# A Strassen-type SwiGLU stage on one Trainium2 core: gate/up and down products merged into one block

## The chip, the cores and the metric

The program runs on one core of one Trainium2 chip. It is one launch; the time is the device time of that launch in microseconds (us). The engines named below are TensorE (PE, matmuls, with its weight loads as PEld), VectorE (DVE), ScalarE (ACT), GpSimd (POOL) and SyncE (SP, which here only issues transfers). Each runs its own list of instructions in order and meets the others through semaphores.

## The reference

One layer of an encoder trunk is applied to two requests of 2048 and 512 tokens with 1024 features. In short:

```
u = rmsnorm(h) ; z = u @ w_in                       # input projection
a, p, f = short conv with gates, multiscale pool, 2-D Fourier transform of parts of z
h = h + concat(rms(a), rms(p), rms(f)) * mix_g @ w_out
v = rmsnorm(h)
gate, up = split(v @ w_gate_up)                     # 1024 -> 2 * 2816
h = h + (silu(gate) * up) @ w_down                  # 2816 -> 1024
out = rmsnorm(h)                                    # without the 16 meta tokens
```

All of it is in 32-bit floats. The change touches only the last three lines: the two products of the feed-forward part, the product of `silu(gate)` and `up` between them, and the final norm.

## The kernel before

**Three matmuls for one.** Every large product is done with operands split into a high part (type fp32r, an ACT copy) and a low part (what is left, a DVE subtraction). `split_product` (lines 79 to 83) issues hi·hi, hi·lo and lo·hi, which are the lines L81, L82 and L83 of all rows below.

**Seven products for eight.** Both feed-forward products cut their matrices in 2 x 2 and use seven products (`FORMS = 7`, numbered 0 to 6) of sums of quadrants. The summed weights (`gu_sums`, `down_sums`) are made beforehand in HBM by accumulating transfers that POOL issues in eight "waves" (class `Forms`). The sums of `v`, the normed activations, are made on chip: `v_raw` holds the quadrants A11, A21, A22, A12 and one sum, and DVE makes four subtractions in it in place (`v_sum`), named D, N6, E and S3.

**`gateup`** (from L1463). The tokens come in three "halves" of 428, 428 and 424 columns. For each half there are 11 iterations of two output tiles y = 0 and 1, so 33 iterations; each has 14 units, ordered by form and then by y. A unit is one form of one tile: 12 matmuls of 428 columns. SP loads one 256 KB weight block per unit into a ring of eight (`gu_raw`); ACT makes `gu_hi` and DVE makes `gu_lo`, six units ahead of PE. In a new half ACT and DVE also make `v_form_hi` and `v_form_lo` of each of the seven forms (`v_split`, 1712 columns each), and DVE the four sums. These big steps are put in the last iteration of the half before, one form after another. ACT and DVE also read the accumulators out (`read_out`): s1 is a copy of form 0; u2, u3, c22, c12, c21 are DVE sums of accumulators; then two SiLUs on ACT, two products (`act_left`, `act_right`) and four sums (`act_sums`) on DVE. POOL stores seven forms of the result to `act_forms` in HBM. PE waits where an accumulator is used again, or where the next form is added onto it: form 3 waits for u2, form 4 for s1, form 5 for c22, form 6 for u3.

**`down`** (from L1720) is a block of its own: it begins when all engines have left `gateup`. It has 3 groups of token tiles (4, 3 and 3 tiles of 128 tokens per side), 77 units each: for a unit SP loads 256 KB of weights (`down_raw`) and up to 256 KB of activations (`act_raw`), ACT and DVE split both, PE does 12 (or 9) matmuls of 512 columns, and DVE adds the seven accumulated forms onto the residual rows `h_tiles`. After the first eight units' loads SP issues the load of `final` and the eight first residual tiles (L1837, L1853), and only then the loads of the ninth unit. ACT, POOL and DVE do the final norm, POOL stores the rows.

The order of the work on every engine is written out by hand by these loops; no scheduler moves anything.

Of the kernel before, what the change touches and what calls it, by code (L numbers as in the profile page):

```python
# [1462 lines left out]
def gateup(nc, c, gu, dn, w_landed):  # L1463

    HM, SLOTS, AHEAD = max(HALVES), UNIT_RING, 6
    ITER, UNITS = GU_ITER, GU_UNITS
    A11, A21, A22, A12, AX = range(5)
    D_, N6, E_, S3 = range(1, 5)
    a_of, b_of, c_of = (lambda y: 3 * y), (lambda y: 3 * y + 1), (lambda y: 3 * y + 2)
    ACC = (a_of, b_of, c_of, b_of, a_of, c_of, b_of)
    with ExitStack() as ctx:
        sb = lambda n, s, d=F32: ctx.enter_context(nc.sbuf_tensor(n + "_sb", s, d))
        sem = lambda n: ctx.enter_context(nc.semaphore(n))
        vf_hi, vf_lo = (sb(n, [P, FORMS, 4, HM], F32R) for n in ("v_form_hi", "v_form_lo"))  # L1480
        vraw = sb("v_raw", [P, 5, 4, HM])
# [628 lines left out]
```

## Time and profile before

| what | us |
|---|---|
| median of 3 runs (lowest, highest) | 2551.2 (2550.27, 2556.29) |
| the profiled execution, its own time | 2553.51 |
| its span from first to last instruction | 2551.9 |
| PE busy in it | 2398.7 (94%) |
| DVE busy | 1550.0 (61%) |
| ACT busy | 893.4 (35%) |
| POOL busy | 359.6 (14%) |

The span is 1.6 us shorter than the execution's own time: what lies around it. The stages follow each other: input projection up to about 475 us, Fourier transform to 600, output projection to 868, gate/up from 897 to 1983, down from 2007 to about 2540, and the end of the final norm and the last stores to 2552. A busy share says that an engine works, not that it sets the time; what sets it in a stage is the engine for which nothing else waits, and its idle stretches are what a change can win.

### The profile page before, as it was taken

The page shows a single profiled execution, that of the slowest core. Times are in us where ns is not written, and L with a number is a line of the kernel's source. Part 1 is how long each engine was busy: PE and PEld are TensorE (multiplying, and loading weights), DVE is VectorE, ACT ScalarE, POOL GpSimd, SP SyncE. Part 2 cuts the span into 40 slices and gives each one's busy share as a digit, 9 for nine tenths or more (in the row PEclk, how much of TensorE's full clock was granted, in tenths as well). Part 3 has the DMA queues.
Part 4 walks back from the last instruction along what each step waited for, and adds up shares of the span by engine and source line. Part 5 has one row for each costly group of instructions (what it writes and reads, how often), then busy time and mean ns, then how long its engine had stood idle before and what let it go on. Part 6 is the DMA issues. An engine that isn't in the chain of part 4 may idle for free. (4 is left out here: it accounts for less than half of the span.)

```text
span 2551.9 us, 32577 instructions
## 1 busy us (share of the span) xinstructions
PE 2398.7 (94%) x11786; PEld 2150.5 (84%) x11786; DVE 1550.0 (61%) x2312; ACT 893.4 (35%) x1486; POOL 359.6 (14%) x509
## 2 busy tenths in 40 slices
PE   6999999788999589999999999999999599999997
PEld 4887888677888489999999999999999488888886
DVE  4443545555877375555865555856555375686875
ACT  4121211142443243333433333433333243454543
POOL 0110110006444001111010011111111000110101
PEclk9999999887999799999999999999999799999999
DMA  5656871265565547888555455455553786687874
GB/s 179 215 134 161 220 201 52 91 208 190 210 251 199 187 142 259 259 251 250 163 192 199 159 163 161 155 164 160 163 160 118 251 281 192 207 311 225 260 242 139
DMA packets 216058, 492.95 MB, mean 193 GB/s; under 512 B 27552, under 2 KB 60866, under 8 KB 207469
## 3 DMA queue, kind: packets, MB, share of 16 engines
q1 hardware_dynamic: 188301, 358.99, 43.0%
q0 software_dynamic: 27616, 132.11, 17.3%
q8 instruction: 85, 1.39, 0.2%
q14 instruction: 56, 0.46, 0.1%
HBM read 395.90 MB, written 164.31 MB: 220 GB/s over the span
## 5 line engine op out<-in xcount | busy, mean ns | idle before, releaser
L81 PE MATMUL gu_bank<-v_form_hi_sb,gu_hi_sb 128*128 128x428 f32 (+1 forms) x1848 | 658.5, 356 | 37.7 <-DVE gu_lo_sb L1604 29.8
L82 PE MATMUL gu_bank<-v_form_lo_sb,gu_hi_sb 128*128 128x428 f32 (+1 forms) x1848 | 658.0, 356 | 0.0
L83 PE MATMUL gu_bank<-v_form_hi_sb,gu_lo_sb 128*128 128x428 f32 (+1 forms) x1848 | 657.9, 356 | 0.0
L1604 DVE TENSOR_TENSOR gu_lo_sb<-gu_raw_sb,gu_hi_sb 128x512 fp32r<-128x512 f32 x462 | 313.8, 687 | 208.3 <-ACT gu_hi_sb L1556 208.3
L81 PEld LDWEIGHTS gu_bank<-v_form_hi_sb,gu_hi_sb 128*128 128x128 f32 x1848 | 347.3, 188 | 51.2 <-DVE gu_lo_sb L1604 38.2
L1556 ACT ACTIVATE gu_hi_sb<-gu_raw_sb 128x512 fp32r<-128x512 f32 x462 | 281.3, 627 | 254.9 <-PE gu_bank L83 246.8
L82 PEld LDWEIGHTS gu_bank<-v_form_lo_sb,gu_hi_sb 128*128 128x128 f32 x1848 | 347.5, 188 | 11.2
L83 PEld LDWEIGHTS gu_bank<-v_form_hi_sb,gu_lo_sb 128*128 128x128 f32 x1848 | 347.5, 188 | 10.7
L81 PE MATMUL down_bank<-down_hi_sb,act_hi_sb 128*128 128x512 f32 x770 | 301.0, 391 | 27.6 <-DVE act_lo_sb L1943 27.6
L82 PE MATMUL down_bank<-down_lo_sb,act_hi_sb 128*128 128x512 f32 x770 | 300.5, 390 | 0.0
L83 PE MATMUL down_bank<-down_hi_sb,act_lo_sb 128*128 128x512 f32 x770 | 300.5, 390 | 0.0
L1940 DVE TENSOR_TENSOR down_lo_sb<-down_raw_sb,down_hi_sb 128x1024 fp32r<-128x1024 f32 x116 | 141.7, 1222 | 170.2 <-ACT down_hi_sb L1892 169.6
L1892 ACT ACTIVATE down_hi_sb<-down_raw_sb 128x1024 fp32r<-128x1024 f32 x116 | 122.9, 1060 | 296.7 <-PE down_bank L83 238.3
L81 PE MATMUL proj_bank<-u_hi_sb,w_in_hi_sb 128*128 128x512 f32 x480 | 188.6, 393 | 7.7 <-DVE u_lo_sb L459 6.7
L81 PEld LDWEIGHTS down_bank<-down_hi_sb,act_hi_sb 128*128 128x128 f32 x770 | 145.2, 189 | 58.5 <-DVE down_lo_sb L1940 28.3
L82 PE MATMUL proj_bank<-u_lo_sb,w_in_hi_sb 128*128 128x512 f32 x480 | 187.9, 391 | 0.0
L83 PE MATMUL proj_bank<-u_hi_sb,w_in_lo_sb 128*128 128x512 f32 x480 | 187.7, 391 | 0.0
L1541 POOL DMA_DIRECT2D act_forms<-act_left_sb x66 | 36.4, 551 | 984.2 <-DVE act_sums_sb L1654 984.2
L83 PEld LDWEIGHTS down_bank<-down_hi_sb,act_lo_sb 128*128 128x128 f32 x770 | 145.1, 188 | 30.4
L82 PEld LDWEIGHTS down_bank<-down_lo_sb,act_hi_sb 128*128 128x128 f32 x770 | 145.2, 189 | 30.1
L81 PE MATMUL out_bank<-w_panel_hi_sb,v_hi_sb 128*128 128x512 f32 x320 | 128.4, 401 | 5.5 <-DVE h_sb L1347 5.5
L1943 DVE TENSOR_TENSOR act_lo_sb<-act_raw_sb,act_hi_sb 128x384 fp32r<-128x384 f32 (+1 forms) x231 | 132.3, 599 | 0.7 <-ACT act_hi_sb L1899 0.5
(187 smaller groups left out, 3293.2 us busy)
## 6 DMA issues: line engine op xcount, KB each, us to landing
gu_raw_sb<-gu_sums SPq DMA_DIRECT2D x264, 256.0 KB, 3.9
gu_raw_sb<-w_gu_q SPq DMA_DIRECT2D x198, 256.0 KB, 2.6
gu_sums<-w_gu_q POOLq DMA_DIRECT2D x24, 1408.0 KB, 14.4
down_raw_sb<-down_sums SPq DMA_DIRECT2D x132, 256.0 KB, 3.7
act_raw_sb<-act_forms SPq DMA_DIRECT2D x154, 192.0 KB, 3.6
down_raw_sb<-w_down_q SPq DMA_DIRECT2D x99, 256.0 KB, 3.3
w_raw_sb<-w_panels SPq DMA_DIRECT2D x40, 512.0 KB, 3.5
act_raw_sb<-act_forms SPq DMA_DIRECT2D x77, 256.0 KB, 4.3
```

Source lines behind the costliest of these rows:

```text
L81: pe.matmul(out, w[0], x[0], start=first, stop=False, skip_group_check=True)
L82: pe.matmul(out, w[0], x[1], start=False, stop=False, skip_group_check=True)
L83: return pe.matmul(out, w[1], x[0], start=False, stop=last, skip_group_check=True)
L1541: pool.dma_start(c["act_forms"][f, m, :, at:at + n], src[:, 0:n]).then_inc(a_stored, 16)
L1556: act.activation(w_hi[:, s, :], raw[:, s, :], ACT.Copy).then_inc(w_hi_made, 1)
L1604: dve.tensor_tensor(w_lo[:, s, :], raw[:, s, :], w_hi[:, s, :].bitcast(F32), ALU.subtract)\
L1892: act.activation(w_hi[:, s:e, :], w_raw[:, s:e, :], ACT.Copy).then_inc(w_hi_made, 1)
L1940: dve.tensor_tensor(w_lo[:, s:e, :], w_raw[:, s:e, :], w_hi[:, s:e, :].bitcast(F32), ALU.subtract)\
L1943: dve.tensor_tensor(a_lo[:, s, 0:w], a_raw[:, s, 0:w], a_hi[:, s, 0:w].bitcast(F32), ALU.subtract)\
```

## The change

`gateup` and `down` become one function, `swiglu`, with one block. What it does:

- The weight ring (`gu_raw`, `gu_hi`, `gu_lo`) serves both products, with semaphores counted on. The buffers that only the down product needs lie over buffers that only gate/up needs: `act_raw` and `act_hi` over `v_raw`, `act_lo` over the first forms of `v_form_lo`, the residual tiles `h_even` over `v_form_hi`, `h_odd` and `final` over the rest of `v_form_lo`. So the loads and splits of the first down units stand in the lists of SP, ACT and DVE right behind the last gate/up units, and the loads of `final` and `h_even` wait until PE has done all gate/up units.
- The seventh product (form 6) has its own bank for each y (`g_of`), and the order of the forms is 0, 4, 6, 1, 2, 3, 5 (`TURN`). The read-out of c21 moves from behind form 6 to behind form 3, between u3 and c22; form 5 comes directly behind form 3. The form's sign change is gone, so its low part is a plain subtraction.
- The four loads of `v` are issued one by one (A11, two weight blocks, A12, two weight blocks, A21 and A22; in later halves in iterations 2, 4, 6 and 8), and each has its own semaphore. D and N6 are made after form 4's split, E after form 6's, S3 after form 1's; before, D, N6 and E all stood behind form 0's.
- The waves of the `w_down` sums are issued one piece in each of 16 iterations, where before there were two pieces in each of 8.
- The accumulators of the down product are mapped to other banks (`acc`), so that the first form's do not meet the last ones of gate/up.

The core of the diff:

```diff
-    ACC = (a_of, b_of, c_of, b_of, a_of, c_of, b_of)
+    g_of = lambda y: 6 + y
+    ACC = (a_of, b_of, c_of, b_of, a_of, c_of, g_of)
+    TURN = (0, 4, 6, 1, 2, 3, 5)
+    AT = tuple(TURN.index(f) for f in range(FORMS))
...
+            for u in range(GU_UNITS):
...
+                if u == 1:
+                    v_load(0, A12)
+                elif u == 3:
+                    v_load(0, A21)
+                    v_load(0, A22)
+                if i % HF in V_LOAD_AT and f == 0 and y == 0 and i // HF + 1 < len(HALVES):
+                    sp.wait_ge(v_lo_made, FORMS * (i // HF + 1))
+                    v_load(i // HF + 1, V_LOAD_AT[i % HF])
...
+                sp.wait_ge(w_lo_made, w_lo_by(u - SLOTS))
+                sp.dma_start(raw[:, slot(u), :], down_weights(u)).then_inc(w_landed[slot(u)], 16)
...
+                if u == SLOTS - 1:
+                    sp.wait_ge(used, GU_UNITS)
+                    sp.dma_start(gf[:, :], c["final_rows"]).then_inc(gf_landed, 16)
+                    h_load(0)
...
-                if 1 <= i <= 8:
-                    for piece in range(dn.pieces):
-                        dn.wave(pool, i - 1, piece)
+                if 1 <= i <= 8 * dn.pieces:
+                    dn.wave(pool, (i - 1) // dn.pieces, (i - 1) % dn.pieces)
...
             def v_step(k, f):
 
                 v_split(k, f)
-                if f == 0:
+                if f == 4:
                     v_sum(k, D_)
                     v_sum(k, N6)
+                elif f == 6:
                     v_sum(k, E_)
                 elif f == 1:
                     v_sum(k, S3)
...
                 elif f == 3:
                     dve.wait_ge(used, u + 1)
-                    dve.tensor_tensor(u3[:, y, 0:n], acc, s1[:, y, 0:n], ALU.subtract).then_inc(u3_made, 1)
+                    dve.tensor_tensor(u3[:, y, 0:n], there, s1[:, y, 0:n], ALU.subtract).then_inc(u3_made, 1)
                     dve.wait_ge(u3_made, now)
+                    dve.tensor_tensor(s1[:, y, 0:n], bank[:, g_of(y), 0:n], u3[:, y, 0:n], ALU.subtract).then_inc(c21_made, 1)
+                    dve.wait_ge(c21_made, now)
                     dve.tensor_tensor(u3[:, y, 0:n], bank[:, c_of(y), 0:n], u3[:, y, 0:n], ALU.add).then_inc(c22_made, 1)
...
-                elif f == 6:
-                    dve.wait_ge(used, u + 1)
-                    dve.tensor_tensor(s1[:, y, 0:n], s1[:, y, 0:n], acc, ALU.subtract).then_inc(c21_made, 1)
...
             def w_split(u):
-                if u >= UNITS:
+                if u >= GU_UNITS:
+                    splits(u - GU_UNITS)
                     return
```

Three places show how the lists change. First ACT, in its order, at the beginning of gate/up, from the fourth form's high part on (`s1_sb<-gu_bank` is the copy of form 0's accumulator; `gu_used` is PE's count of finished units). Before:

```order
L1565 ACTIVATE v_form_hi_sb<-v_raw_sb 128x1712 [waits v_landed]
L1556 ACTIVATE gu_hi_sb<-gu_raw_sb 128x512 [waits unit_landed6]
L1575 ACTIVATE s1_sb<-gu_bank 128x428 [waits gu_used]
L1556 ACTIVATE gu_hi_sb<-gu_raw_sb 128x512 [waits unit_landed7]
L1575 ACTIVATE s1_sb<-gu_bank 128x428 [waits gu_used]
```

And after:

```order
L1724 ACTIVATE v_form_hi_sb<-v_raw_sb 128x1712 [waits v_summed] x4
L1714 ACTIVATE gu_hi_sb<-gu_raw_sb 128x512 [waits unit_landed6]
L1733 ACTIVATE s1_sb<-gu_bank 128x428 [waits gu_used]
L1714 ACTIVATE gu_hi_sb<-gu_raw_sb 128x512 [waits unit_landed7]
L1733 ACTIVATE s1_sb<-gu_bank 128x428 [waits gu_used]
L1714 ACTIVATE gu_hi_sb<-gu_raw_sb 128x512 [waits gu_used,unit_landed0]
L1738 ACT_TABLE_LOAD
```

The copy s1 stands behind all seven high parts in both. What moved is who waits for it: before it was the ninth and tenth unit of PE (form 4), now it is the third and fourth.

Second DVE, in the last iteration of a half, where the next half's forms are made (`v_raw_sb<-v_raw_sb` are the sums D, N6, E, S3; L1663 and L1863 are u2; L1666 and L1866 are u3; L1668 and L1870 are c22; L1868 is c21). Before:

```order
L1663 TENSOR_TENSOR u_sb<-gu_bank,s_sb 128x428
L1626 TENSOR_TENSOR v_form_lo_sb<-v_raw_sb,v_form_hi_sb 128x1712
L1616 TENSOR_TENSOR v_raw_sb<-v_raw_sb 128x1712 x3
L1604 TENSOR_TENSOR gu_lo_sb<-gu_raw_sb,gu_hi_sb 128x512
L1663 TENSOR_TENSOR u_sb<-gu_bank,s_sb 128x428
L1604 TENSOR_TENSOR gu_lo_sb<-gu_raw_sb,gu_hi_sb 128x512
L1626 TENSOR_TENSOR v_form_lo_sb<-v_raw_sb,v_form_hi_sb 128x1712
L1616 TENSOR_TENSOR v_raw_sb<-v_raw_sb 128x1712
L1604 TENSOR_TENSOR gu_lo_sb<-gu_raw_sb,gu_hi_sb 128x512 x2
L1666 TENSOR_TENSOR u_sb<-gu_bank,s_sb 128x428
L1668 TENSOR_TENSOR u_sb<-gu_bank,u_sb 128x428
```

And after, from the second form's low part to c22 of y = 0:

```order
L1824 TENSOR_TENSOR v_form_lo_sb<-v_raw_sb,v_form_hi_sb 128x1712
L1818 TENSOR_TENSOR v_raw_sb<-v_raw_sb 128x1712 x2
L1806 TENSOR_TENSOR gu_lo_sb<-gu_raw_sb,gu_hi_sb 128x512 x2
L1863 TENSOR_TENSOR u_sb<-gu_bank,s_sb 128x428
L1824 TENSOR_TENSOR v_form_lo_sb<-v_raw_sb,v_form_hi_sb 128x1712
L1818 TENSOR_TENSOR v_raw_sb<-v_raw_sb 128x1712
L1806 TENSOR_TENSOR gu_lo_sb<-gu_raw_sb,gu_hi_sb 128x512
L1863 TENSOR_TENSOR u_sb<-gu_bank,s_sb 128x428
L1806 TENSOR_TENSOR gu_lo_sb<-gu_raw_sb,gu_hi_sb 128x512
L1824 TENSOR_TENSOR v_form_lo_sb<-v_raw_sb,v_form_hi_sb 128x1712
L1818 TENSOR_TENSOR v_raw_sb<-v_raw_sb 128x1712
L1806 TENSOR_TENSOR gu_lo_sb<-gu_raw_sb,gu_hi_sb 128x512 x2
```

behind which, with nothing between:

```order
L1866 TENSOR_TENSOR u_sb<-gu_bank,s_sb 128x428
L1868 TENSOR_TENSOR s_sb<-gu_bank,u_sb 128x428
L1870 TENSOR_TENSOR u_sb<-gu_bank,u_sb 128x428
L1824 TENSOR_TENSOR v_form_lo_sb<-v_raw_sb,v_form_hi_sb 128x1712
L1806 TENSOR_TENSOR gu_lo_sb<-gu_raw_sb,gu_hi_sb 128x512
```

The two u2 stand further back against the new forms, and all four sums and four low parts now lie ahead of the first c22.

Third SP, at the end of gate/up. Before (the two branches are the end of one block and the beginning of the next):

```order
L1528 DMA gu_raw_sb<-gu_sums 128x512 x2
L1477 UNCONDITIONAL_BRANCH
L1828 UNCONDITIONAL_BRANCH
L1847 DMA down_raw_sb<-w_down_q 128x512
L1850 DMA act_raw_sb<-act_forms 128x512
```

And after:

```order
L1625 DMA gu_raw_sb<-w_gu_q 128x512 x2
L1652 DMA gu_raw_sb<-w_down_q 128x512
L1660 DMA act_raw_sb<-act_forms 128x512
```

The branches are gone and the loads of the first down units follow the last of gate/up. The load of `final` (L1664) and the eleven pieces of the residual tiles (L1643) still stand between the loads of the eighth and of the ninth down unit.

## Rows read from the trace of the kernel before

**Rows 1.** The page, costliest groups: shapes, count | busy us, mean ns | idle before, releaser.
```profile
L1556 ACT ACTIVATE gu_hi_sb<-gu_raw_sb 128x512 fp32r<-128x512 f32 x462 | 281.3, 627 | 254.9 <-PE gu_bank L83 246.8
```

**Rows 2.** Waits of PE: line, released by; us in total, times, longest.
```profile
PE gu_bank L81 <- DVE u_sb L1663: 6.6, 5, 2.8
...
PE gu_bank L81 <- DVE u_sb L1668: 1.3, 2, 0.7
```

**Rows 3.** Timeline, beginning of gate/up: start, duration, instruction, idle before.
```profile
875.75 2.24 SPq L1519 DMA_DIRECT2D v_raw_sb<-vT  x4
...
887.54 1.63 ACT L1565 ACTIVATE v_form_hi_sb<-v_raw_sb 128x1712 fp32r<-128x1712 f32 x1 [19.08 <-DMA v_raw_sb<-vT]
...
889.20 1.94 DVE L1626 TENSOR_TENSOR v_form_lo_sb<-v_raw_sb,v_form_hi_sb 128x1712 fp32r<-128x1712 f32 x1 [22.84 <-ACT v_form_hi_sb L1565]
891.06 5.76 DVE L1616 TENSOR_TENSOR v_raw_sb<-v_raw_sb 128x1712 f32<-128x1712 f32 x3
...
897.48 0.72 PE L81 MATMUL gu_bank<-v_form_hi_sb,gu_hi_sb 128*128 128x428 f32 x1 [29.76 <-DVE gu_lo_sb L1604]
...
915.87 0.43 PE L81 MATMUL gu_bank<-v_form_hi_sb,gu_hi_sb 128*128 128x428 f32 x1 [2.77 <-DVE u_sb L1663]
```

**Rows 4.** Windows: stretch, length; busy PE, PEld, DVE, ACT, POOL; clock, DMA share, GB/s.
```profile
877.90:887.10 9.20, 0.00 (x0) 0.00 (x0) 0.00 (x0) 0.00 (x0) 0.00 (x0) 0.50 1.04 385
897.48:900.50 3.02, 3.02 (x9) 2.81 (x10) 3.02 (x3) 3.02 (x5) 0.00 (x0) 0.50 0.55 174
913.10:915.87 2.77, 0.00 (x1) 0.03 (x1) 2.77 (x6) 0.63 (x1) 0.00 (x0) 1.00 0.19 48
```

**Rows 5.** Timeline, change from the first half to the second.
```profile
1252.79 0.53 ACT L1580 ACTIVATE silu_sb<-gu_bank 128x428 f32<-128x428 f32 x1 [1.28 <-PE gu_bank L83]
...
1255.00 0.60 DVE L1668 TENSOR_TENSOR u_sb<-gu_bank,u_sb 128x428 f32<-128x428 f32 x1
...
1255.75 0.43 PE L81 MATMUL gu_bank<-v_form_hi_sb,gu_hi_sb 128*128 128x428 f32 x1 [0.68 <-DVE u_sb L1668]
```

**Rows 6.** Timeline, read-out of form 3 in the middle of gate/up, DVE.
```profile
1508.73 0.60 DVE L1666 TENSOR_TENSOR u_sb<-gu_bank,s_sb 128x428 f32<-128x428 f32 x1 [3.23 <-PE gu_bank L83]
...
1509.37 0.60 DVE L1668 TENSOR_TENSOR u_sb<-gu_bank,u_sb 128x428 f32<-128x428 f32 x1
...
1509.89 0.68 DVE L1604 TENSOR_TENSOR gu_lo_sb<-gu_raw_sb,gu_hi_sb 128x512 fp32r<-128x512 f32 x1
...
1511.05 0.60 DVE L1666 TENSOR_TENSOR u_sb<-gu_bank,s_sb 128x428 f32<-128x428 f32 x1 [0.47 <-PE gu_bank L83]
```

**Rows 7.** Timeline, from gate/up to down.
```profile
2006.62 0.43 SPq L1853 DMA_DIRECT2D final_sb<-final_rows  x1
...
2007.48 0.77 PE L81 MATMUL down_bank<-down_hi_sb,act_hi_sb 128*128 128x512 f32 x1 [24.90 <-DVE act_lo_sb L1943]
...
2031.87 1.06 ACT L1892 ACTIVATE down_hi_sb<-down_raw_sb 128x1024 fp32r<-128x1024 f32 x1 [16.81 <-DMA act_raw_sb<-act_forms]
...
2034.94 0.47 PE L81 MATMUL down_bank<-down_hi_sb,act_hi_sb 128*128 128x512 f32 x1 [2.72 <-DVE act_lo_sb L1943]
```

**Rows 8.** Windows of the same place, columns as in rows 4.
```profile
2006.62:2031.87 25.25, 24.39 (x96) 19.90 (x96) 8.61 (x12) 6.30 (x9) 0.00 (x0) 0.87 1.04 336
1998.27:2006.62 8.35, 0.00 (x0) 0.00 (x0) 1.11 (x1) 2.10 (x3) 0.00 (x0) 0.50 0.85 276
1986.00:1993.00 7.00, 0.00 (x0) 0.00 (x0) 0.69 (x2) 0.00 (x0) 3.74 (x7) 0.50 0.60 217
2007.48:2012.90 5.42, 5.42 (x13) 4.26 (x14) 4.45 (x6) 4.20 (x6) 0.00 (x0) 0.50 1.06 404
...
2040.00:2060.00 20.00, 20.00 (x90) 16.56 (x89) 19.02 (x29) 10.47 (x15) 0.00 (x0) 1.00 0.85 303
```

**Rows 9.** An idle stretch of PE in the input projection and the clock behind it.
```profile
228.83 1.97 PE L628 MATMUL proj_bank<-ident_sb,x_tiles_sb 128*128 128x128 f32 x8 [4.25 <-DVE u_lo_sb L459]
228.83:238.10 9.27, 7.68 (x22) 6.08 (x23) 1.92 (x3) 1.20 (x2) 0.00 (x0) 0.50 0.67 244
```

More of the change, by code:

```diff
@@ L1460, in _, with row_ranges, swiglu @@
             transposes(NBLK - 1, 24 * (NBLK - 1) + 16)
-def gateup(nc, c, gu, dn, w_landed):
+def row_ranges(pair, right):
+    out, lo = [], P * pair
+    for at, n, token in zip(SEQ_AT, HALVES, TOKEN_AT):
+        a, b = max(lo, at), min(lo + P, at + n)
+        if a < b:
+            out.append((a - lo, b - lo, token + a - at + (n if right else 0)))
+    return out
+def swiglu(nc, c, gu, dn, half, eps):
     HM, SLOTS, AHEAD = max(HALVES), UNIT_RING, 6
-    ITER, UNITS = GU_ITER, GU_UNITS
+    ITER, UNITS = GU_ITER, FORMS * HF
+    ALL = UNITS * len(PAIRS)
     A11, A21, A22, A12, AX = range(5)
@@ L1510, in gateup, with slot, unit_landed, w_lo_by @@
         V_SUM = (0, N6, E_, D_, 0, S3, 0)
+        V_LOAD_AT = {2: A11, 4: A12, 6: A21, 8: A22}
+        def slot(u):
+            return (GU_UNITS + u) % SLOTS
+        def unit_landed(u):
+            earlier = len(range(slot(u), GU_UNITS, SLOTS))
+            return 16 * earlier + 32 * ((GU_UNITS + u) // SLOTS + 1 - earlier)
+        def w_lo_by(u):
+            return GU_UNITS + (u // 2 if u >= 0 else u) + 1
+        def acc(g, i):
+            return bank[:, ((6, 7, 0, 3), (2, 5, 1, 4))[g % 2][i], :]
@@ L1523, in _, with v_load @@
-            v_load(0)
+            def v_load(k, where):
+                n = HALVES[k]
+                row, at = {A11: (0, 0), A21: (0, n), A22: (512, n), A12: (512, 0)}[where]
+                sp.dma_start(vraw[:, where, :, 0:n], c["vT"][row:row + 512, TOKEN_AT[k] + at:TOKEN_AT[k] + at + n]
+                             .rearrange("(k p) n -> p k n", p=P)).then_inc(v_landed[where], 16)
+            v_load(0, A11)
             gu.all_made(sp)
-            for u in range(UNITS):
+            for u in range(GU_UNITS):
@@ L1595, in _ @@
                     v_split(i // HF + 1, f)
+            for u in range(ALL):
+                k, v = divmod(u, UNITS)
+                splits(u + AHEAD)
+                if 70 <= v < 70 + PAIRS[k][1]:
+                    square_rows(k, 0, v - 70)
+                if k and 4 <= v < 4 + PAIRS[k - 1][1]:
+                    square_rows(k - 1, 1, v - 4)
+            for i in range(PAIRS[-1][1]):
+                square_rows(len(PAIRS) - 1, 1, i)
         @block.vector
@@ L1599, in w_split @@
             def w_split(u):
-                if u >= UNITS:
+                if u >= GU_UNITS:
+                    splits(u - GU_UNITS)
                     return
@@ L1613, in v_sum @@
                     dve.wait_ge(v_summed, 4 * k + what - 1)
-                else:
-                    dve.wait_ge(v_landed, 64 * (k + 1))
+                for where in {D_: (A11, A21), N6: (A22,), E_: (), S3: (A12,)}[what]:
+                    dve.wait_ge(v_landed[where], 16 * (k + 1))
                 dve.tensor_tensor(part(out), part(x), part(y), ALU.subtract).then_inc(v_summed, 1)
@@ L1658, in read_out @@
                 n, now = HALVES[i // HF], 2 * i + y + 1
-                acc = bank[:, ACC[f](y), 0:n]
+                there = bank[:, ACC[f](y), 0:n]
                 if f == 1:
@@ L2018, in build @@
             outproj(nc, c, feed, ident, half, eps)
-        landed = [ctx.enter_context(nc.semaphore(f"unit_landed{i}")) for i in range(UNIT_RING)]
-        gateup(nc, c, gu, dn, landed)
-        down(nc, c, dn, landed, half, eps)
+        swiglu(nc, c, gu, dn, half, eps)
 def dft_tables(length, rows, freqs):
```

457 lines of the change are left out of this document (208 added, 249 removed).

## The prediction

> **What bounds the kernel now.** I read the busy shares first: PE 94%, DVE 61%, so most of the time is PE's own, and only PE's idle stretches and its slow clock can be won. Then PE's waits, longest first. Two stand out, both between stages: 29.76 us before the first gate/up matmul [rows 3] and 24.90 us before the first down matmul [rows 7]. Behind these come 2.77 us at the seventh gate/up unit [rows 3], 2.72 us at the ninth down unit [rows 7], and small waits for u2 and c22 [rows 2]: 6.6 + 1.3 us, less the 2.77, is 5.1 us, all at the two changes of half. Everywhere else in gate/up and down PE waits for nothing. The clock adds to both large waits: it restarts at 0.50, that is 1.2 of 2.4 GHz, for 3.02 us in gate/up [rows 4] and for 5.42 us in down [rows 8], which loses half of that, 1.5 and 2.7 us.
>
> So two units of time serve below. A gate/up unit takes 2.32 to 2.33 us (read-outs of neighbouring units start 2.32 apart [rows 6]); a down unit of four tiles takes 2.66 (90 matmuls in 20 us, twelve to the unit [rows 8]).
>
> **From gate/up to down (gain).** PE's last gate/up matmul ends at 2007.48 - 24.90 = 1982.58. Now the first eight down units are loaded and split by then: their weights follow in a ring that ran eight units ahead, their activations are those of the first two halves, stored long ago, and the banks they need are read out by form 5 of the tile. PE goes on without a gap, at full clock, and the eight units end 8 x 2.66 = 21.3 us later. Then the ninth. Its loads stand on SP behind `final` and eleven pieces of residual tiles, 4.7 MB, and these now wait for PE's last gate/up matmul, because the buffers lie over `v_form_hi` and `v_form_lo`. Before, from the issue of `final` at 2006.62 to the split of the ninth unit's operands at 2031.87 were 25.25 us at 336 GB/s, 8.5 MB [rows 7, 8]. In it were 1.9 MB left from the sixteen loads of 4.2 MB, of which 2.3 MB had moved (8.35 us at 276 GB/s); these are now gone. New is the store of the last iteration's seven act forms, 7 us at 217 GB/s, 1.5 MB, which before had ended when down began [rows 8] and now runs beside the residual tiles. So 8.1 MB, 24.1 us at the same rate, and 3.1 from the split to PE's start (2031.87 to 2034.94 [rows 7]): the ninth unit starts 27.3 us after the last gate/up matmul, a stall of 6.0 us. At 404 GB/s, the best rate seen there [rows 8], it would be 23.2 us, a stall of 1.9. A stall of 6 us also drops the clock, which after 4.25 idle us was at 0.50 [rows 9]; I take 2.0 us for the restart, between 1.5 and 2.7. Before, the ninth unit came 2034.94 - 1982.58 = 52.4 us after; now 29.3. Gain 23.1 us; 29 at best, 20 at worst (rate 300 GB/s).
>
> The Trainium skill, "DMA: Bandwidth & Descriptors", section "Queues, rings and completion order", says that each transfer engine takes turns between the queues that have work for it. By this the stores of POOL's queue share with SP's loads; if instead they ran only behind them, the ninth unit would come 1.5 MB earlier and the stall would be about 1.5 us. No row of before has both at once at this place.
>
> **The beginning of gate/up (no gain).** Here the words of the change promise most: PE can start when A11 has landed. The four v loads moved at 385 GB/s from 877.9 to 887.1 [rows 4], and ACT took them up at 887.54 [rows 3]. A11 alone (0.88 MB) lands at about 880.7, ACT's high part takes 1.63, DVE's low part 1.94, then one weight block: PE starts at about 885 instead of 897.48. But form 4 now comes second and is added onto form 0's bank, so PE's third unit waits for s1, and in ACT's list s1 stands behind all seven high parts. The last of them waits for S3 on DVE. DVE's chain: A22 now has four weight blocks ahead of it and lands at 877.9 + 4.56 MB / 385 GB/s + 0.5 = 890.2. Behind it N6 1.92, two weight splits 1.2, low part 1.86, E 1.92, two splits 1.2, low part 1.86, S3 1.94 (back-to-back instructions overlap by 0.08: 889.20 to 891.06 for 1.94 [rows 3]) end at 902.1. ACT: high part 1.63, one weight part 0.6 [rows 1], s1 0.5, and 0.2 to PE: 905. PE has had two units and idles some 13 us, so the clock is at half again. The seventh unit starts four units later, 905 + 9.3 + 2.0 for the clock = 916.4; before it was at 915.87 [rows 3]. Its own wait for u2 is gone, since form 1 comes there. Cost 0.5 us; between 4 lost (A22 later, clock 2.7) and 3 won (A22 as before).
>
> **Changes of half (loss).** Before, DVE was late by 5.1 us in both together. Now follow DVE in the last tile of a half, from its first unit's start T. ACT gets to form 4's high part when the fourth unit is done: 4 x 2.33 = 9.3, 0.2 to see it, a SiLU 0.45, high part 1.53, weight part 0.6, DVE's weight split 0.6: DVE begins form 4's low part at T + 12.8. From there to c22 of y = 0 stand, by the order shown, three low parts 5.6, four sums 7.6, six weight splits 3.6, two u2 1.0, and u3, c21, c22 with 0.64, 0.64 and 0.60 [rows 6]: 19.7 us. PE needs it 0.2 later (1255.60 to 1255.75, and a first matmul of 0.43 [rows 5]): T + 32.7. The unit that waits (form 5, y = 0) is the thirteenth and due at T + 28.0: 4.6 us late. Its twin waits for c22 of y = 1: 0.52, low part 1.86, split 0.6, 1.9 for three read-outs, less 0.6 and less a unit: 1.9 us. Together 6.5 for each change, where 2.6 were; the same reckoning for before gives 3.1 where 2.6 is measured, so I take 6.2. If the 4.6 us also drop the clock, the slow unit mostly hides in the second wait; 0.4 for that. Two changes: 13.2 against 5.1, 8.1 us lost. Bounds: 3 lost, if ACT delivers earlier, and 14, if the clock falls for 9.27 us as in rows 9.
>
> The Trainium skill, "TensorE: Matmul & The Clock Gate", section "HAM oscillation — how this bites in real kernels", warns that waits between bursts of matmuls drop the clock again each time. This speaks against a change that turns many short waits into a few of 4 to 13 us. Rows 9 agree for 4.25 us; 2.77 us left the clock at 1.00 [rows 4]. By this rule the second half-change wait costs more and the sum would be some 3 us worse.
>
> **Every other iteration (near nothing, but on a knife's edge).** c22 now has u3 and c21 ahead of it and only one unit's time. u3 starts 0.22 after the next unit does: the wait at 1255.75 began at 1255.07, a free successor starts 0.17 before that end, a unit earlier is 1252.57, and ACT's read-out there began at 1252.79 [rows 5]. c22 of y = 0 ends 0.22 + 1.88 = 2.10 into the unit, PE has it at 2.32 of 2.33. For y = 1 a weight split comes between: 0.22 + 1.28 + 0.52 + 0.60 + 1.88 = 4.50, plus 0.23 = 4.73 of 4.66: 0.07 late, 33 times 2 us in all. Taken 2; bounds 0 and, with 0.3 lost in each of 66 units, 20.
>
> **Nothing by themselves:** the spread v loads of later halves (they end four iterations before use), the spread waves of the `w_down` sums (PE has no wait there [rows 2]), the plain subtraction for form 6 (1.94 either way), the bank map, fewer SP instructions. The waves' cover is some sixteen further iterations of 32 us.
>
> **Sum.** 23.1 - 0.5 - 8.1 - 2.0 = 12.5 us. The profiled execution took 2553.5 (span 2551.9 and 1.6 around it), so 2541.0 for that one; it lay 2.3 above the median of the runs, 2551.2, which gives 2538.7. I forecast 2539 us.
>
> **Rivals.**
> 1. *The front work is hidden after all.* Half changes cost no more than before and the start wins 3, the stall of the ninth unit is 2 us. For it: DVE is 61% busy only, and the sums are spread. Against it: in the order all four sums stand ahead of the first c22. 29 + 3 - 1 = 31 at most, 2520; typically 2524.
> 2. *The ninth unit and its followers.* The 8.1 MB move at 276 GB/s, as the first down loads did [rows 8]: the ninth unit comes 32.5 us after the last gate/up matmul, and the next pairs stall 2 us more. For it: DMA share 1.04 there [rows 8]. Against it: the 336 measured with the same tiles. Gain only 52.4 - 32.5 - 4 = 16, and 10 to 14 lost in gate/up: 2545 to 2549.
> 3. *Slower: the c22 chain.* If u3 to c22 takes 0.3 to 0.6 us longer than rows 6 let expect, because the weight split ahead of u3 isn't done when the unit ends, each of 66 units of form 5 waits that long: 20 to 40 us, against 14.5 won elsewhere. From 0.22 us per unit the gain is gone; at 0.45 the time is 2567. For it: the margin is 0.01 us. Against it: ACT has the weights two units ahead.
> 4. *It doesn't do what it says*: down still starts after a gap, since one of the shared buffers is released late. Then the 24.9 us stay and 2560 follows.
>
> **How the numbers follow.** Forecast 0.56 (2531 to 2544), rival 1 0.18, rival 2 0.15, rival 3 0.07, rival 4 0.04. Range 2526 to 2548, which leaves out the better half of rival 1 and most of 3 and 4. About 0.3%, 7.7 us, can be told from no change. Faster by more (below 2543.5): all of rival 1, nearly all of the forecast and a little of rival 2, 0.76; within it: the rest of these, and the mild end of rival 3, 0.16; slower 0.08.
>
> **What would show it.** In the profile after: no PE wait at the first down unit and one of 2 to 8 us, for act_lo, at the ninth; two early units at about 885, then some 13 us of wait for s1, and the seventh unit at 914 to 919; two pairs of waits for c22 of about 4.5 and 1.9 us; no other wait over 0.2 us in gate/up. Half-change waits under 3 us, or an s1 wait that is missing, would make the forecast too high; waits of 0.3 us in every iteration, too low.

## The result: faster by a little over a quarter of a per cent, and the profile after

| | kernel before | kernel after |
|---|---|---|
| median of 20 runs (lowest, highest), us | 2554.73 (2547.02, 2562.26) | 2547.03 (2540.06, 2557.29) |
| the profiled execution, us | 2553.51 | 2544.79 |
| ratio, with its 95% interval | | 0.9973 [0.9963, 0.9982] |

The gain is 7.7 us by the medians and 8.7 by the two profiled executions; 12.5 were forecast. The time forecast, 2539, is 8 us too low: 3.5 of that are the kernel before, whose three first runs had their median at 2551.2 and whose twenty have it at 2554.7; the rest, 12.5 less 7.7, is an error of the sum.

PE's longest waits after the change (line, released by: us in total, times, longest). They answer to [rows 2] and to the waits in [rows 3, 7]:

```profile
PE gu_bank L81 <- DVE gu_lo_sb L1806: 17.3, 1, 17.3
...
PE gu_bank L81 <- ACT s_sb L1733: 13.7, 1, 13.7
PE gu_bank L81 <- DVE u_sb L1870: 9.2, 4, 4.4
...
PE gu_bank L81 <- DVE act_lo_sb L1898: 3.5, 1, 3.5
```

The wait of 24.90 us before down is gone, and the one of 29.76 before gate/up is now two, 17.3 and 13.7. The same waits on the timeline, with the first down matmul:

```profile
906.67 0.69 PE L81 MATMUL gu_bank<-v_form_hi_sb,gu_hi_sb 128*128 128x428 f32 x1 [13.72 <-ACT s_sb L1733]
...
918.19 0.36 PE L81 MATMUL gu_bank<-v_form_hi_sb,gu_hi_sb 128*128 128x428 f32 x1
...
1263.20 0.70 PE L81 MATMUL gu_bank<-v_form_hi_sb,gu_hi_sb 128*128 128x428 f32 x1 [4.36 <-DVE u_sb L1870]
...
1993.80 0.35 PE L83 MATMUL gu_bank<-v_form_hi_sb,gu_lo_sb 128*128 128x424 f32 x1
1993.99 0.39 PE L81 MATMUL gu_bank<-gu_hi_sb,act_hi_sb 128*128 128x512 f32 x1
...
2019.66 0.47 PE L81 MATMUL gu_bank<-gu_hi_sb,act_hi_sb 128*128 128x512 f32 x1 [3.52 <-DVE act_lo_sb L1898]
```

918.19 is the seventh unit, which now follows without a wait. The clock behind these waits (columns as in [rows 4]):

```profile
906.67:912.00 5.33, 5.33 (x17) 5.01 (x18) 4.62 (x5) 3.27 (x6) 0.00 (x0) 0.56 0.13 33
1263.20:1270.00 6.80, 6.55 (x25) 5.92 (x26) 6.70 (x9) 0.89 (x2) 0.00 (x0) 0.77 0.32 95
1628.78:1636.00 7.22, 7.22 (x23) 6.63 (x24) 7.12 (x9) 0.89 (x2) 0.00 (x0) 0.57 0.31 92
2019.66:2026.00 6.34, 6.34 (x21) 5.04 (x22) 5.49 (x8) 5.12 (x8) 0.00 (x0) 0.73 1.05 386
```

And the row that the forecast had nothing for. Down in mid-flow, no wait in it and the clock at 1.00 throughout; first the kernel before, then the one after:

```profile
2200.00:2250.00 50.00, 50.00 (x222) 41.39 (x221) 35.72 (x45) 28.45 (x49) 13.79 (x24) 1.00 0.79 253
2300.00:2350.00 50.00, 50.00 (x222) 41.42 (x221) 32.30 (x47) 23.05 (x37) 0.00 (x0) 1.00 0.73 229
```

```profile
2200.00:2250.00 50.00, 50.00 (x220) 41.02 (x219) 40.72 (x56) 26.31 (x44) 12.46 (x20) 1.00 0.76 255
2300.00:2350.00 50.00, 50.00 (x220) 41.04 (x219) 31.84 (x46) 23.20 (x37) 0.00 (x0) 1.00 0.73 225
```

222 matmuls in 50 us before, 220 after. Averaged over the start times of a longer stretch, one follows the other in 226.7 ns before and 228.9 after; below this is called the distance. The engine is busy all the time in both, so neither busy time nor waits show it; only the counts in equal windows do. Over the 2,214 matmuls from the ninth unit on it is 4.9 us.

**The account of the 8.7 us** by which the two profiled executions differ, from the times of PE's rows:

| stretch | us won |
|---|---|
| stages ahead of gate/up (nothing differs there: chance) | -0.6 |
| beginning of gate/up (seventh unit at 918.19, where it was 915.87, less the 0.6) | -1.7 |
| from the seventh unit to the end of gate/up (1075.8 us up to the first down matmul at 1993.99, before 1066.7) | -9.1 |
| from there to the ninth down unit (25.7 us, before 52.4) | +26.7 |
| slow clock behind that (6.34 us at 0.73) | -1.7 |
| distance of the down matmuls | -4.9 |

### The profile page after: what moved, and what is told of

It reads as the page before. It is cut to its first block and busy times, and to the rows that moved or that the text cites. A ratio compares the mean times of both kernels' runs of the same rounds, so it can differ in the third digit from the quotient of the medians.

```text
span 2543.2 us, 32577 instructions
## 1 busy us (share of the span) xinstructions
PE 2408.1 (95%) x11786; PEld 2151.0 (85%) x11786; DVE 1548.3 (61%) x2312; ACT 903.1 (36%) x1486; POOL 361.0 (14%) x509
## 5 line engine op out<-in xcount | busy, mean ns | idle before, releaser
L81 PE MATMUL gu_bank<-v_form_hi_sb,gu_hi_sb 128*128 128x428 f32 (+1 forms) x1848 | 663.2, 359 | 40.2 <-DVE gu_lo_sb L1806 17.3
L81 PE MATMUL gu_bank<-gu_hi_sb,act_hi_sb 128*128 128x512 f32 x770 | 303.9, 395 | 3.5 <-DVE act_lo_sb L1898 3.5
L83 PE MATMUL gu_bank<-gu_hi_sb,act_lo_sb 128*128 128x512 f32 x770 | 302.4, 393 | 0.0
L82 PE MATMUL gu_bank<-gu_lo_sb,act_hi_sb 128*128 128x512 f32 x770 | 299.7, 389 | 0.0
L1893 DVE TENSOR_TENSOR gu_lo_sb<-gu_raw_sb,gu_hi_sb 128x1024 fp32r<-128x1024 f32 x116 | 141.4, 1219 | 157.2 <-ACT gu_hi_sb L1750 157.2
L1750 ACT ACTIVATE gu_hi_sb<-gu_raw_sb 128x1024 fp32r<-128x1024 f32 x116 | 122.5, 1056 | 295.4 <-PE gu_bank L83 258.3
L83 PEld LDWEIGHTS gu_bank<-gu_hi_sb,act_lo_sb 128*128 128x128 f32 x770 | 145.0, 188 | 33.9
L81 PEld LDWEIGHTS gu_bank<-gu_hi_sb,act_hi_sb 128*128 128x128 f32 x770 | 145.2, 189 | 33.0 <-DVE gu_lo_sb L1893 3.9
L82 PEld LDWEIGHTS gu_bank<-gu_lo_sb,act_hi_sb 128*128 128x128 f32 x770 | 144.8, 188 | 32.3
```

The costliest lines, as they stand in the source:

```text
L81: pe.matmul(out, w[0], x[0], start=first, stop=False, skip_group_check=True)
L82: pe.matmul(out, w[0], x[1], start=False, stop=False, skip_group_check=True)
L83: return pe.matmul(out, w[1], x[0], start=False, stop=last, skip_group_check=True)
L1750: act.activation(w_hi[:, s:e, :], raw[:, s:e, :], ACT.Copy).then_inc(w_hi_made, 1)
L1893: dve.tensor_tensor(w_lo[:, s:e, :], raw[:, s:e, :], w_hi[:, s:e, :].bitcast(F32), ALU.subtract)\
```

## The experiments

The stages ahead of gate/up end up to 9 us apart from run to run, though nothing in them differs. So I compare, beside the medians, the stretch from PE's last row of 32 transposes in the output projection to the end of the span. The two rows, before and after:

```profile
862.29 5.42 PE L1423 MATMUL out_bank<-ident_sb,stage_sb 128*128 128x128 f32 x32 [2.04 <-DVE stage_sb L1354]
```

```profile
862.93 5.40 PE L1423 MATMUL out_bank<-ident_sb,stage_sb 128*128 128x128 f32 x32 [2.04 <-DVE stage_sb L1354]
```

Call the stretch R: 1689.6 us before, 1680.3 after. It comes from the one profiled execution of each kernel.

**1. The kernel before once more.**

> The kernel before, unchanged, profiled once more. In its first profile neighbouring down matmuls start 0.2267 us apart; in the profile of the changed kernel 0.2290 us, which over some 2,200 matmuls is 5 us that my sum did not have. If the kernel sets this distance (its addresses or its accumulator banks), it is 0.2267 here again. If it differs from execution to execution or from chip to chip, it will be another number here, anywhere from 0.226 to 0.230.

2547.43 us, R 1688.0, PE's waits as in [rows 2, 3, 7] within 0.6 us, except 1.40 for 2.77 at the seventh gate/up unit and 1.32 for 2.72 at the ninth down unit; down distance 226.7 ns again. So for this kernel R repeats to 2 us, and the distance to 0.1 ns. For two kernels below the medians say less than R does; both numbers are given there.

**2. The residual tiles two units later.**

```
-                if u == SLOTS - 1:
+                if u == SLOTS + 1:
                     sp.wait_ge(used, GU_UNITS)
                     sp.dma_start(gf[:, :], c["final_rows"]).then_inc(gf_landed, 16)
                     h_load(0)
```

> The changed kernel, but the loads of final and of the first residual tiles stand on SP two units later, behind the loads of the tenth down unit. My account: the wait of 3.5 us at the ninth down unit and the slow clock behind it (1.7 us) go, about 5 us less than the changed kernel, 12 us less than before (ratio to before about 0.9953), unless the eleventh unit waits in their place. Rival: the transfers are limited by bandwidth alone, so the wait only moves two units on and the time stays (0.997). If the layout sets the distance of the down matmuls, it is 0.2290 us here too.

2537.5 us (4 runs), ratio 0.9931 [0.9905, 0.9957], R 1674.2. PE no longer waits in down at all. 6.1 us less than the kernel after in R: the wait of 3.5, the slow clock of 1.7, and 0.9 at the second change of half, where one iteration took 38.75 us here and 39.67 in the kernel after. That 0.9 is chance: with the same order of gate/up experiment 3 had 38.72 there and experiment 7 had 39.77. So the ninth unit did wait behind `final` and the residual tiles, and the whole wait was a matter of order on SP. The distance stays at 228.9.

**3. Down's bank map of before.**

```
-            return bank[:, ((6, 7, 0, 3), (2, 5, 1, 4))[g % 2][i], :]
+            return bank[:, 4 * (g % 2) + i, :]
...
```

PE's waits ahead of the first units of down are adapted to it.

> The changed kernel with the accumulators of the down product in the banks of before (0 to 3 and 4 to 7 in turn), everything else as changed. If the bank map makes the down matmuls slower, their distance goes back from 0.2290 to 0.2267 us and down is 5 us shorter. If the addresses in SBUF or the execution itself do it, 0.2290 stays, or whatever the others of this call show.

2548.69 us, R 1680.6, distance 228.9: the banks have no part in it.

**4. The one block with gate/up's order of before.** `TURN` is 0 to 6, form 6 is back in form 3's bank and last, D, N6 and E stand behind form 0, the four `v` loads of a half go together (each keeps its own semaphore).

```
-    ACC = (a_of, b_of, c_of, b_of, a_of, c_of, g_of)
-    TURN = (0, 4, 6, 1, 2, 3, 5)
+    ACC = (a_of, b_of, c_of, b_of, a_of, c_of, b_of)
+    TURN = (0, 1, 2, 3, 4, 5, 6)
...
-                if f == 4:
+                if f == 0:
                     v_sum(k, D_)
...
```

> Only the merged block: gate/up has its order of before (forms 0 to 6, seventh product in the bank of the second, c21 behind form 6, D, N6 and E behind form 0, the v loads all at once), while rings, overlaid buffers, down banks and spread sums are those of the changed kernel. My account of the two profiles: the order of forms and sums costs 9 to 11 us in gate/up (two changes of half 7, read-outs 1.5, beginning 1 to 2), the merged block wins 25. So this kernel should be 9 to 11 us faster than the changed one and 17 below before, ratio 0.9930 to 0.9940, with waits of about 1.0, 0.7 and 1.0 us at each change of half as before. Rival: the new order costs nothing by itself and the missing gain lies in down; then it is as the changed kernel, 0.997.

2533.8 us (8 runs), ratio 0.9927 [0.9906, 0.9947], R 1663.9. Its rows:

```profile
878.41 1.63 ACT L1720 ACTIVATE v_form_hi_sb<-v_raw_sb 128x1712 fp32r<-128x1712 f32 x1 [12.12 <-DMA v_raw_sb<-vT]
...
888.35 0.72 PE L81 MATMUL gu_bank<-v_form_hi_sb,gu_hi_sb 128*128 128x428 f32 x1 [22.75 <-DVE gu_lo_sb L1803]
...
906.74 0.43 PE L81 MATMUL gu_bank<-v_form_hi_sb,gu_hi_sb 128*128 128x428 f32 x1 [2.53 <-DVE u_sb L1862]
...
1999.38 0.76 PE L81 MATMUL gu_bank<-gu_hi_sb,act_hi_sb 128*128 128x512 f32 x1 [4.10 <-DVE act_lo_sb L1898]
```

At the changes of half PE waits 1.02, 0.69 and 0.96 us, and 0.94, 0.64 and 0.95, as before the change. The new order of gate/up, with its spread loads and the bank of the seventh product, therefore costs 16.4 us of R, two thirds of the 25.7 that this kernel gains on the one before. The medians say less of both: 13.2 us between this kernel and the one after, and by the ratio 19 (14 to 24) against the one before. This profiled execution was a quick one, 2525.39 where the median is 2533.8, so the merge is worth 19 to 26 us and the order costs 13 to 16; experiment 8 has the order alone at 14.

Half of the 16.4 is at the start, which I had put at 0.5: the seventh unit stands 46.8 us behind the row of transposes, 55.3 in the kernel after, and 53.6 in the kernel before. The 6.8 us by which this start beats that of before I put down to the semaphores: ACT takes up A11 18.5 us behind the transposes, at 878.41, when one load has landed; before it was 25.2 us behind, at 887.54 [rows 3], when all four had. These 6.7 us are the whole difference, but no run changes the semaphores alone.

**5. Down's buffers at the places of after, in the kernel before.**

```
-        w_raw, a_raw = (sb(n, [P, SLOTS, UNIT]) for n in ("down_raw", "act_raw"))
-        w_hi, w_lo, a_hi, a_lo = (sb(n, [P, SLOTS, UNIT], F32R) for n in ("down_hi", "down_lo", "act_hi", "act_lo"))
-        h = sb("h_tiles", [P, 2, 2, 4, D])
+        w_raw = sb("down_raw", [P, SLOTS, UNIT])
+        w_hi, w_lo = (sb(n, [P, SLOTS, UNIT], F32R) for n in ("down_hi", "down_lo"))
...
+        sb("gap_1", [P, 9312 // 4])
+        a_raw = sb("act_raw", [P, SLOTS, UNIT])
+        a_hi = sb("act_hi", [P, SLOTS, UNIT], F32R)
+        h_even = sb("h_even", [P, 2, 4, D])
+        sb("gap_2", [P, 16640 // 4])
+        a_lo = sb("act_lo", [P, SLOTS, UNIT], F32R)
...
```

> The kernel before, with the down block's rings and residual tiles at the places in SBUF that they have after the change (weights' high and low parts at 33,696 and 50,080 bytes, activations' at 108,640 and 174,432); nothing else differs. My theory is that these places are what makes the distance between down's matmuls 228.9 ns instead of 226.7: then it is 228.9 here, and the profiled time some 4.8 us above the 2547 to 2553 of the kernel before. The rival: the distance comes with the one block (one long program for PE), whatever the places; then it stays at 226.7 and so does the time.

2553.22 us, R 1693.0, which is 3.4 to 5.0 above the two of before; distance 228.9:

```profile
2200.00:2250.00 50.00, 50.00 (x220) 41.02 (x219) 35.93 (x46) 29.20 (x49) 13.89 (x24) 1.00 0.80 258
2300.00:2350.00 50.00, 50.00 (x220) 41.04 (x219) 31.25 (x45) 23.22 (x37) 0.00 (x0) 1.00 0.71 226
```

The places alone make it. The rival, the one long program, is out: this kernel has the two blocks.

**6. The weights alone at their new place.**

```
-        w_raw, a_raw = (sb(n, [P, SLOTS, UNIT]) for n in ("down_raw", "act_raw"))
-        w_hi, w_lo, a_hi, a_lo = (sb(n, [P, SLOTS, UNIT], F32R) for n in ("down_hi", "down_lo", "act_hi", "act_lo"))
+        w_raw = sb("down_raw", [P, SLOTS, UNIT])
+        w_hi, w_lo = (sb(n, [P, SLOTS, UNIT], F32R) for n in ("down_hi", "down_lo"))
+        a_raw = sb("act_raw", [P, SLOTS, UNIT])
+        a_hi, a_lo = (sb(n, [P, SLOTS, UNIT], F32R) for n in ("act_hi", "act_lo"))
```

> The kernel before, with one change of place in down: the weights' high and low parts at 33,696 and 50,080 bytes, where the kernel after has them, instead of 50,080 and 66,464; the activations' stay at 82,848 and 99,232. If the place of the operand that streams (the weights) sets the distance, it is 228.9 ns; if that of the stationary one (the activations), or the distance of the two, whose offset stays a multiple of 16,384 here, it is 226.7. If the places have no part in it at all, 226.7 too.

2549.16 us, R 1689.7, distance 226.7. Moved by 16,384 bytes, the weights alone change nothing.

**7. The kernel after with two pads.**

```
+        sb("pad_1", [P, 832 // 4])
         with ExitStack() as first:
...
             vf_hi = early("v_form_hi", [P, FORMS, 4, HM], F32R)
+            early("pad_2", [P, 1792 // 4])
             vf_lo = early("v_form_lo", [P, FORMS, 4, HM], F32R)
...
```

> The kernel after, with two pads (832 and 1792 bytes), so that the activations' high and low parts in down stand at a multiple of 2,048 bytes from the weights', as they do in the kernel before (there of 16,384). If what counts is that offset, the distance of down's matmuls falls from 228.9 to 226.7 ns and the time by some 4.8 us, to about 2540. If it is another property of the places, or the one block, it stays at 228.9 and 2545 to 2549.

2541.03 us, R 1675.1: 5.2 less than after, with the same waits (4.37 at the first change of half, 3.94 at the ninth unit). The windows count as before the change:

```profile
2200.00:2250.00 50.00, 50.00 (x222) 41.42 (x221) 40.22 (x54) 26.24 (x44) 12.36 (x20) 1.00 0.78 255
2300.00:2350.00 50.00, 50.00 (x222) 41.42 (x221) 32.90 (x49) 22.74 (x37) 0.00 (x0) 1.00 0.73 228
```

So it is shown from both sides, by 5 and 7, that the place of the activations' buffers makes the difference.

What about the place does it is not settled. The kernels lay buffers one behind the other, so the addresses can be worked out: in every kernel here down's weights stand 416 bytes above a multiple of 512. The activations do so too wherever the distance is 226.7; where it is 228.9 they stand 96 and 352 bytes above one. Both readings fit: that the offset between the two operands has to be a multiple of 512, or that only the activations' own address counts. A run with both rings moved by 64 bytes would tell them apart; there is none.

**8. The new gate/up in a block of its own.** The changed lists of SP, POOL, ACT, DVE and PE for gate/up, before's buffers, then before's `down`:

```
-            for f in range(FORMS):
+            for q, f in enumerate(TURN):
...
         gateup(nc, c, gu, dn, landed)
         down(nc, c, dn, landed, half, eps)
```

> The new gate/up (order of forms, seventh product in banks of its own, split v loads, spread sums) in a block of its own, with the kernel before's boundary and its down block. My theory, from the comparison of the two traces: the new gate/up costs 1.6 at the start and 9.4 over the iterations and half changes, and nothing else changes: 11 us slower than before, about 2564, with 24 to 25 us of wait at the first down matmul, waits of 4.4 us at each change of half and of 13 to 14 us for s1 at the start, and 226.7 ns between down's matmuls. The rival: part of those 11 us comes from the shared block (other places of the buffers, other pads of time); then this kernel is within 3 us of before, and the waits at the half changes are under 3 us.

2567.93 us (5 runs), ratio 1.0057 [1.0036, 1.0078]; R 1703.6, 14.0 above before. From the transposes to the last gate/up matmul it takes 9.1 us more than before (1129.3, before 1120.3). The other 5 us I had not expected: they stand in the boundary.

```profile
2023.67 0.76 PE L81 MATMUL down_bank<-down_hi_sb,act_hi_sb 128*128 128x512 f32 x1 [29.50 <-DVE act_lo_sb L1946]
```

24.90 before [rows 7]. The last read-outs and stores, now behind form 5, have little part in it: POOL issues its first store 4.9 us behind the last gate/up matmul, where it was 4.4. The rest lies behind the stores, in a stretch in which no engine works and nothing moves, 9.9 us long here and 5.2 before. The last store's issue, the first load's issue, and the stretch as a window (columns as in [rows 4]); first this kernel, then the one before:

```profile
2002.22 0.54 POOL L1548 DMA_DIRECT2D act_forms<-act_right_sb  x1
...
2014.91 0.33 SPq L1850 DMA_DIRECT2D down_raw_sb<-w_down_q  x1
```

```profile
2005.00:2014.90 9.90, 0.00 (x0) 0.00 (x0) 0.00 (x0) 0.00 (x0) 0.00 (x0) 0.50 0.00 0
```

```profile
1990.22 0.54 POOL L1541 DMA_DIRECT2D act_forms<-act_right_sb  x1
...
1998.27 0.33 SPq L1847 DMA_DIRECT2D down_raw_sb<-w_down_q  x1
```

```profile
1993.00:1998.20 5.20, 0.00 (x0) 0.00 (x0) 0.00 (x0) 0.00 (x0) 0.00 (x0) 0.50 0.00 0
```

From the last store's issue to down's first load it is 12.7 us here and 8.05 before, and 8.06 when the kernel before ran again. Why the change of block takes 4.6 us longer here is not known. Without the merge the new order is a loss.

**9. v forms at a pitch of 448 columns** (in the kernel after).

```
+        sb("pad_1", [P, 80])
...
-            vf_hi, vf_lo = (early(n, [P, FORMS, 4, HM], F32R) for n in ("v_form_hi", "v_form_lo"))
+            early("pad_2", [P, 16])
+            vf_hi, vf_lo = (early(n, [P, FORMS, 4, 448], F32R) for n in ("v_form_hi", "v_form_lo"))
...
```

> The kernel after, with the stored forms of v at a pitch of 448 columns instead of 428 (the matmul still takes 428 or 424), and two pads. So in gate/up each block of v forms stands at a multiple of 256 bytes from each block of weights (before at multiples of 16 only), and in down each activation block at a multiple of 512. If the offset between the two operands decides, as the runs on down showed, gate/up's matmuls follow each other in about 191.8 ns instead of 194.1 (the same 2.3 ns less, over 5,544 matmuls: 12.7 us) and down's in 226.7 instead of 228.9 (4.8 us), less what new waits give back: PE goes faster than DVE's chain for c22 can follow, with 28 ns less to a unit, so I expect 5 to 10 of the 12.7 us at worst to be lost there and a time of 2529 to 2538. If the rule holds for down's shape alone, gate/up stays at 194 and the time is 2540 to 2543. If it needs a multiple of 512 bytes, half of the blocks gain and the distance is about 193.

2544.43 us (10 runs), ratio 0.9966 [0.9953, 0.9979], R 1674.2: 6.1 us below the kernel after by R, and only 2.6 by the medians. Down ran at 226.7 ns, here with the high parts at offsets that are a multiple of 512 bytes but not of 2,048. Gate/up did not gain. An iteration of 428 columns takes 32.53 to 32.93 us, that is 193.6 to 196.0 ns for a matmul; in the kernel after it is 32.64 to 32.67, or 194.3 to 194.5. This window has 257 matmuls, where the kernel after has 260; from 1400 to 1450 it is 260 against 259:

```profile
1500.00:1550.00 50.00, 50.00 (x257) 48.23 (x256) 29.17 (x49) 17.50 (x31) 7.51 (x14) 1.00 0.60 196
```

My extension of the rule to gate/up fell. An offset of 512 bytes instead of 256 does not save it: at this pitch every second block of v forms stands at a multiple of 512 from the weights, and in experiment 11, which has the same places, its matmuls are as slow as those of its neighbours, 196.0 ns each in the second half. In the first half, with the same buffers, all of them have 193.0 to 193.6. So the place alone does not decide in gate/up, and what does is open.

**10. s1 ahead of the later v forms** (in the kernel after, on ACT).

```
+                if q == 2:
+                    read_out(0)
+                    read_out(1)
             for u in range(GU_UNITS):
                 w_split(u + AHEAD)
-                read_out(u)
+                if u > 1:
+                    read_out(u)
```

> The kernel after, with one thing moved: at the start of gate/up ACT reads form 0's two banks into s1 ahead of the high parts of the last four v forms, not behind them. My prediction's claim: PE's third unit waits (13.7 us) only because s1 stands behind seven high parts in ACT's list. Then that wait falls to about 3 us, form 6 follows at once, and the seventh unit waits for form 1's low part instead, some 5 us; it starts at 905 to 910 instead of 918, and the time falls by 8 to 10 us, to about 2537. The rival: DVE's chain (low parts, sums and weight splits, 26 us of work) bounds the start whatever ACT's order; then the seventh unit still starts at 915 or later, and the time is that of the kernel after within 2 us.

2537.22 us (5 runs), ratio 0.9944 [0.9927, 0.9961], R 1674.2.

```profile
892.98 0.43 PE L81 MATMUL gu_bank<-v_form_hi_sb,gu_hi_sb 128*128 128x428 f32 x1 [2.51 <-DVE gu_lo_sb L1810]
...
907.79 0.72 PE L81 MATMUL gu_bank<-v_form_hi_sb,gu_hi_sb 128*128 128x428 f32 x1 [5.29 <-DVE gu_lo_sb L1810]
```

13.7 us of waiting became 2.5 and 5.3, as expected, and the seventh unit stands 47.1 us behind the transposes instead of 55.3. Of these 8.2 R shows 6.1: the wait of 5.3 drops the clock once more (0.63 from 907.79 to 914.00, 2.3 us). The wait was a matter of one position in ACT's list.

**11 and 12. What the runs point to, together.** The one block, gate/up's order of before, the residual tiles two units later, and round offsets; first with the pitch of 448, then with 428 and the pads of experiment 7.

> The one block of the change with the order of gate/up of the kernel before (seventh product in form 3's bank and last, DVE's sums of v behind form 0, the v loads of a half together; each v load still with a semaphore of its own), the residual tiles loaded two units later in down, and v forms at a pitch of 448 columns with the pads. From the runs so far: the order of before in one block gave 2534; the tiles later gave 9 us and more to the kernel after, of which I count 6 to 9 here; the offsets 4.8 in down and up to 12.7 in gate/up. So 2508 to 2519. If gate/up's distance doesn't change, 2520 to 2524. If gate/up at a faster pace runs into waits on DVE, above 2519 with waits in every iteration.

2522.95 us (4 runs), ratio 0.9871 [0.9846, 0.9896], R 1657.3, no wait in down.

> As the last kernel (one block, order of gate/up of the kernel before, residual tiles two units later, down's operands at offsets of a multiple of 2,048 bytes), but with the v forms at their pitch of 428 columns. Counted from the row that precedes gate/up to the end, the version without late tiles and offsets took 1663.9 us of the profiled execution; the offsets should take off 4.8 and the late tiles the 4.1 us of the ninth unit's wait and up to 2 of slow clock behind it: 1653 to 1655, where the version with the pitch of 448 took 1657.2. So 2 to 4 us below its 2523: about 2520. If the pitch of 448 had helped gate/up after all, this one is 2 us or more slower than 2523.

2517.82 us (5 runs), ratio 0.9850 [0.9830, 0.9870], R 1651.8. PE's waits from gate/up on are now all in gate/up:

```profile
PE gu_bank L81 <- DVE gu_lo_sb L1806: 22.7, 1, 22.7
...
PE gu_bank L81 <- DVE u_sb L1865: 6.5, 5, 2.7
...
PE gu_bank L81 <- DVE u_sb L1870: 1.3, 2, 0.7
```

This is the best kernel: 38 us below the kernel before, by R and by the ratio, and 28 below the changed one by R. The pitch of 448 costs 5.5 us of R rather than 2 to 4; with it the seventh unit waited 3.81 us instead of 2.70, and the clock dropped behind that wait.

## Why the gain was forecast too large, and which step failed

**The step that failed** is the one headed "nothing by themselves". It counted only what engines wait for, and so the overlay of buffers stood in the sum as lists and semaphores, at no price. The overlay moves down's operands to 33,696, 50,080, 108,640 and 174,432 bytes, and with that each of the 2,214 remaining matmuls takes 2.2 ns more: 4.9 us (experiments 5 and 7). The layout was in the diff, and the distance of down's matmuls was in the trace, but I took it over as a constant of the shape. The 0.2% of the time that it costs is spread over 500 us, where no wait marks it.

The other terms together came out 1.7 us better than forecast, so that R fell by 12.5 + 1.7 - 4.9 = 9.3. That 12.5 less 4.9 is 7.6 and the medians say 7.7 is therefore partly luck. The terms below missed by 1.9, -1.2, 1.0 and 0.0.

The other terms, in the order of the sum:

- *Gate/up to down, +23.1.* Measured +26.7 less 1.7 for the clock: 25.0. The mechanism held in each part: no wait at the first down matmul, a wait for act_lo at the ninth, 25.7 us behind the last gate/up matmul. I had 27.3, of which 24.1 for 8.1 MB at 336 GB/s, up to ACT's split; it was 22.4 us (1994.18 to 2016.60), at 345 GB/s 7.7 MB. The alternative of a stall near 1.5 us, with POOL's stores behind SP's loads, did not come about. Experiment 2 shows the cause by taking it away.
- *Beginning of gate/up, -0.5.* Measured -1.7. PE at 885.6 for 885, third unit at 906.67 for 905, the seventh at 918.19 for 916.4. DVE's chain was read right. S3 ended at 903.9 for 902.1, because DVE could take up A22 only at 892.2, where I had it landed at 890.2; the clock cost 2.3 for 2.0. What was missed is outside the sum: the same separate semaphores in the old order start 8.5 us earlier (experiment 4).
- *Changes of half, -8.1.* Measured -7.1, from the time between SiLUs of successive iterations. The first late unit waits 4.36 and 4.24 for 4.6. The clock did fall, and the second wait, reckoned at 1.9, shrank to 0.25 and nothing, since the slow units gave DVE its time. I had allowed 0.4 for that. Of the 7.1, 0.9 are the chance of experiment 2.
- *Other iterations, -2.0.* Measured some 2.0 (9.1 less 7.1), but not as I had it. In an iteration without a change of half it is 0.03 to 0.06 us (32.65, before 32.61, at 428 columns), where y = 1 was to cost 0.07: some 1.4 in all. The last iteration costs 0.65 (33.22 us, before 32.57). There the splits of down's first units now stand in the lists of ACT and DVE, and one unit waits 0.34 us for c22; with two blocks (experiment 8) it takes 32.56. The knife's edge held: rival 3 would have shown a wait in every iteration.
- *No effect of the bank map:* right (experiment 3). The spread of the `w_down` waves was not tried by itself.

**The rivals.** Rival 1 (front work hidden): no; 13.7 and 4.4 us of waits were there. Rival 2 (the followers of the ninth unit): no; no unit behind it waits. Its time, 2545 to 2549, is that measured, but by another mechanism, so a right number would have been no evidence for it. Rivals 3 and 4: no. The clock fell behind waits of 3.52, 4.24 and 4.36 us, and was at 1.00 behind 2.53 (experiment 4, from 906.74 to 912.00). The Trainium skill, "TensorE: Matmul & The Clock Gate", section "HAM oscillation — how this bites in real kernels", warns that waits between bursts of matmuls drop the clock again; the three longer waits agree. But the 3 us that this was to add did not come, since a slow unit hid the wait behind it.

## What to carry to other kernels

When a change moves buffers, count matmuls in equal windows of busy stretches before and after: a pace that is 1% slower shows in no wait and no busy share. Where fp32r matmuls of 128x512 follow one another, lay the stationary and the moving ring so that their addresses have the same remainder modulo 512; every layout here that had this was the faster one, though which part of it is needed is not shown. And of a change that bundles a merge with a reordering, try each alone: here the merge was worth 26 us of R (19 by the ratio), and the reordering took 16 of them back (13 by the medians).

## What the runs showed of the hardware that I had not expected

- The distance between matmuls of 128x512 with full clock depends on where the operands lie in SBUF: 226.7 ns with offsets from weights to activations of a multiple of 512 bytes (in four layouts), 228.9 with 74,944, 58,560 and 140,736, which are multiples of 64 and not of 128 (in one layout). Eight profiles have the one, six the other, and none lies between. The offset and the activations' own address were never varied apart, and offsets of 128 or 256 bytes were not tried. Only down's shape was shown to react; for gate/up's 428 columns a pitch with offsets of 256 and 512 bytes made some iterations quicker and some slower (193.3 and 196.0 ns in the two halves of experiment 11), and the whole slower. The mechanism is not known.
- The same output projection, with nothing changed in it or ahead of it, ended between 863.2 and 872.1 in these runs. The twenty executions of one kernel lie up to 17 us apart, so small differences need the medians, or a mark behind that stage; and R of a single execution can itself lie off the medians, by some 7 us here (experiments 4 and 9).
